# Feed-forward as seven block products for both pairs, with the output products spread between the blocks

## What is computed

```python
def swiglu_ffn(h, w1, w3, w2):
    return (jax.nn.silu(h @ w1) * (h @ w3)) @ w2
# h: 512 x 1024; w1, w3: 1024 x 2816; w2: 2816 x 1024
# x = x + gate * swiglu(...)   (first block, with a gate per channel)
# h = h + swiglu_ffn(...)      (second block, two layers)
```

## Time and profile before

| | |
|---|---|
| median of three runs | 2142.71 us (2135.99 to 2143.28) |
| span of the profiled execution | 2133.8 us |
| its own time around the span | not shown; the three runs lie 2.2 to 9.5 us above the span |
| PE busy | 2112.2 us, 99% |
| DVE busy | 1199.0 us, 56% |
| ACT busy | 949.7 us, 45% |
| POOL busy | 906.6 us, 42% |
| mean granted TensorE clock | 0.998 |

### The profile page before, as it was taken

The page is one execution under the profiler, slowest core; times in us unless marked ns, Lnnn a source line. Parts: engine busy times, 40 slices in busy tenths (PEclk is TensorE's granted clock), DMA queues, the critical chain, the costliest instruction groups (busy, mean ns, idle before and its releaser), DMA issues.

```text
span 2133.8 us, 32541 instructions
## 1 busy us (share of the span) xinstructions
PE 2112.2 (99%) x11677; PEld 1779.1 (83%) x11677; DVE 1199.0 (56%) x1776; ACT 949.7 (45%) x1519; POOL 906.6 (42%) x489
## 2 busy tenths in 40 slices
PE   8999999999999999999999999999999999999997
PEld 6888888888888988988878988988888878988986
DVE  3216545643468513546977642753788877742753
ACT  3415555743244423344464432444666754432342
POOL 3332333344435354554754454444333334454443
PEclk9999999999999999999999999999999999999999
DMA  8222222166542232333132233333222122233332
GB/s 311 80 60 60 80 79 69 55 220 210 172 152 89 85 113 89 104 92 114 50 90 89 89 105 98 102 88 110 80 80 79 54 71 83 89 109 95 111 85 73
DMA packets 63826, 216.60 MB, mean 102 GB/s; under 512 B 7105, under 2 KB 8257, under 8 KB 62593
## 3 DMA queue, kind: packets, MB, share of 16 engines
q1 hardware_dynamic: 63744, 215.55, 32.4%
HBM read 213.42 MB, written 2.10 MB: 101 GB/s over the span
## 4 chain that ended last, share of the span: by engine, by line
PE 92%; DVE 3%; ACT 2%; issue 1%; DMA 1%; SPq 0%; DVEq 0%; ACTq 0%
PE ps L660 23%; PE ps L661 23%; PE ps L662 23%; PE ps L1108 4%; PE ps L1107 4%; PE ps L1106 4%; PE ps L889 1%; PE ps L890 1%; PE ps L888 1%; PE ps L983 1%; PE ps L1281 1%; PE ps L993 1%; DMA ada_w<-in_w_ada_first 1%; DMA x_res<-in_x 1%; DVE acc L2320 1%
## 5 line engine op out<-in xcount | busy, mean ns | idle before, releaser
L465 POOL TENSOR_TENSOR w_lo<-w_raw,w_hi 128x1024 fp32r<-128x1024 f32 (+2 forms) x324 | 728.4, 2261 | 874.1 <-ACT w_hi L1415 872.8
L660 PE MATMUL ps<-h_hi,w_lo 128*128 128x512 f32 x1408 | 563.8, 400 | 1.6 <-DVE h_lo L2030 1.2
L661 PE MATMUL ps<-h_lo,w_hi 128*128 128x512 f32 x1408 | 549.1, 390 | 0.0
L662 PE MATMUL ps<-h_hi,w_hi 128*128 128x512 f32 x1408 | 548.6, 390 | 0.0
L1415 ACT ACTIVATE w_hi<-w_raw 128x1024 fp32r<-128x1024 f32 (+2 forms) x324 | 311.6, 975 | 497.3 <-PE ps L662 423.8
L660 PEld LDWEIGHTS ps<-h_hi,w_lo 128*128 128x128 f32 x1408 | 264.5, 188 | 64.2 <-issue 8.4
L662 PEld LDWEIGHTS ps<-h_hi,w_hi 128*128 128x128 f32 x1408 | 264.3, 188 | 56.3
L661 PEld LDWEIGHTS ps<-h_lo,w_hi 128*128 128x128 f32 x1408 | 264.7, 188 | 52.1 <-issue 1.0
L660 PE MATMUL ps<-gu_hi,w_lo 128*128 128x512 f32 x528 | 205.5, 389 | 0.0
L661 PE MATMUL ps<-gu_lo,w_hi 128*128 128x512 f32 x528 | 205.5, 389 | 0.0
L662 PE MATMUL ps<-gu_hi,w_hi 128*128 128x512 f32 x528 | 205.4, 389 | 0.0
(11 more groups left out here) (459 smaller groups left out, 3704.9 us busy)
## 6 DMA issues: line engine op xcount, KB each, us to landing
w_raw<-in_w_ffn_in SPq DMA_DIRECT2D x132, 512.0 KB, 3.6
w_raw<-in_w_hg SPq DMA_DIRECT2D x40, 512.0 KB, 3.6
w_raw<-in_w_ffn_out SPq DMA_DIRECT2D x48, 384.0 KB, 3.2
w_raw<-in_w_conv_gate SPq DMA_DIRECT2D x32, 512.0 KB, 3.5
w_raw<-in_w_merge SPq DMA_DIRECT2D x32, 512.0 KB, 4.6
ada_w<-in_w_ada SPq DMA_DIRECT2D x32, 512.0 KB, 4.5
w_raw<-in_w_ffn_out SPq DMA_DIRECT2D x48, 320.0 KB, 2.9
w_raw<-in_w_cp SPq DMA_DIRECT2D x20, 512.0 KB, 3.6
```

The source lines that it names most:

```text
L465: pool.tensor_tensor(w_lo[s][:, 0:n], raw[s][:, 0:n], w_hi[s][:, 0:n].bitcast(F32), ALU.subtract).then_inc(lo_done[s], 1)
L660: pe.matmul(out, wl, hi, start=first, stop=False)
L661: pe.matmul(out, wh, lo, start=False, stop=False)
L662: return pe.matmul(out, wh, hi, start=False, stop=last)
```

## The change

In all three feed-forwards rounds 0 and 1 stay ordinary, and from round 2 (the third) on both pairs are made as seven block products: 18 steps, `form(r, p)`, per feed-forward, in place of 8 or 9. Each step uses the same four half banks 2, 3, 6 and 7. The output products no longer come in two halves. The products of the round two back (8 tiles of x by two hidden tiles, so 8 groups of 6 matmuls) stand in fours within the two steps of a round, two behind the fourth block product and two behind the seventh, in banks 0, 1, 4 and 5. DVE adds each to x at once. Those of the last two rounds follow behind the last step (`last_outputs`). Weights of the output product get their own buffers (`out_raw`, `out_hi`, `out_lo`). The loops over rounds are written out. The first feed-forward makes both batches of sums of h in round 0. Some semaphores are shared where there were two.

```diff
 # PE, one step
+            def form(r, p):
+                i, o, q = form_step(e, r, p), r - FIRST_FORM, Q_FFI[e] + r
+                former, fr = 1 - p, r - 1 + p
+                if e == 0:
+                    pe.wait_ge(S["ffn_sa"], 2 * pair_no(e, fr, former) + 1)
+                else:
+                    pe.wait_ge(S["ffn_scaled"], scaled(e, fr, former) + 1)
+                if i % FORM_STEPS == 0:
+                    pe.wait_ge(S["ffn_val"], pair_no(e, FIRST_FORM - 1, 1) + 1)
+                    pe.wait_ge(S["side_val"], 2 * KC + 16 * e + 16)
+                pe.wait_ge(S["side_lo"], 1 + 2 * i + 1)
+                term(p, 0, C11, block(0, 0)).then_inc(S["side_mm"], 1)
...
+                term(p, 3, C22, summed(T1)).then_inc(S["side_mm"], 1)
+                out(o, 4 * p)
+                out(o, 4 * p + 1)
+                pe.wait_ge(S["form_kept"], 3 * i + 1)
+                pe.wait_ge(lo_done[2 * p], q + 1)
+                term(p, 0, C11, block(1, 0), add=True)
...
+                term(p, 2, C21, summed(T4), add=True).then_inc(unit_done[2 * p + 1], 1)
+                out(o, 4 * p + 2)
+                out(o, 4 * p + 3)
+            def last_outputs():
+                q = Q_FFI[e] + ROUNDS
+                for half in range(2):
+                    for t in range(2):
+                        s, r = 2 * t + half, ROUNDS - 2 + t
...
+                        for n in range(4 * half, 4 * half + 4):
...
+                            mm = out_tiles(LAST_BANKS[n], n, r, w_hi[s], w_lo[s], t == 0, t == 1)
 # POOL, one step
+                    if not final:
+                        first_form(nr, np_)
...
+                    pool.tensor_tensor(f_lo[p][0], w_12[p], f_hi[p][0].bitcast(F32), ALU.subtract).then_inc(lo_done[2 * p], 1)
...
+                    pool.tensor_tensor(f_lo[p][2], w_22[p], f_hi[p][2].bitcast(F32), ALU.subtract)\
+                        .then_inc(lo_done[2 * p + 1], 1)
...
+                    third_sum_low(nr, np_)
+                    out_low(nr - FIRST_FORM, np_)
 # DVE, ordinary rounds 0 and 1
                     if (r, p) == (0, 1):
-                        batch = 1 if e else 0
-                        terms_sum(batch)
-                        terms_low(batch)
-                    if e == 0 and (r, p) == (1, 1):
+                        if e == 0:
+                            terms_sum(0)
+                            terms_low(0)
                         terms_sum(1)
                         terms_low(1)
+                    if (r, p) == (1, 0):
+                        sum_2(FIRST_FORM, 0)
+                        lows_and_sum_4(FIRST_FORM, 0)
 # DVE, one step: additions to x of the step before, sums and joins, additions, activation
+                if i % FORM_STEPS:
+                    for n in (2, 3):
+                        out_add(o + p - 1, 4 * (1 - p) + n)
...
+                for n in (0, 1):
+                    out_add(o, 4 * p + n)
                 if e:
...
+                    scale_gate(p, r)
+                    scale_up(p, r)
+                value(p, r)
+                low(p, r)
 # DVE, end of a feed-forward
+            for n in (6, 7):
+                out_add(OUT_ROUNDS - 1, n)
+            dve_resid(dve, i, last_done, lambda n: LAST_BANKS[n], gate, **norm)
```

More of the change, by code:

```diff
@@ L63, with form_step, pair_no, scaled @@
 Q_QK, Q_V, Q_GLA, Q_MERGE, Q_MIX = 0, 2, 4, 12, 20
[L64 to L112, removed]
+Q_FFI = [22, 39, 61]
+Q_CPI, Q_CPO, Q_HG, Q_HGO = 34, 37, 51, 59
+Q_END = 73
+def form_step(e, r, p):
+    return FORM_STEPS * e + 2 * (r - FIRST_FORM) + p
+def pair_no(e, r, p):
+    return 2 * (ROUNDS * e + r) + p
+def scaled(e, r, p):
+    return 4 + 2 * (pair_no(e, r, p) - 2 * ROUNDS) if e else 2 * p
+def gu_at(r, p):
+    return 2 * (r % 3) + p
+def out_unit(e, o, n):
+    return OUT_COUNT * e + 8 * o + n
 KB = 1024
@@ L471, in pool_rounds @@
                     pool_lo(pool, s, q, sizes[s])
[L473 to L505, removed]
@@ L1162, in pe_ffn, with out_tiles @@
-            first()
-            for half, (r0, r1) in enumerate(HIDDEN):
-                for r in range(max(r0, 1), WINO_FROM[e][half]):
-                    hidden(r, h_ready(pe, h_base + KC) if (e, r) == (0, 1) else None)
-                with pe.Fori(WINO_FROM[e][half], r1) as r:
-                    winograd(half, r, r + (q_hidden(e, r0) - r0))
-                output(half)
+            def out_tiles(bank, n, r, hi, lo, first, last):
+                for t in range(2):
+                    w, g = slice(t * (D // 2) + n % 4 * P, t * (D // 2) + n % 4 * P + P), gu_at(r, t)
+                    pe.matmul(ps[:, bank, :], lo[:, w], gu_hi[:, g, :], start=(first and t == 0), stop=False)
+                    pe.matmul(ps[:, bank, :], hi[:, w], gu_lo[:, g, :], start=False, stop=False)
+                    mm = pe.matmul(ps[:, bank, :], hi[:, w], gu_hi[:, g, :], start=False, stop=(last and t == 1))
+                return mm
@@ L1674, in act_high, with columns_ahead, act_resid @@
             act.activation(tile(h_hi if out is None else out, n), x[:, n, :], ACT.Copy, scale=gain).then_inc(S["h_hi"], 1)
[L1676 removed]
+        def columns_ahead(q0):
+            return [[(n % 4, q0 + n // 4 + 1)] for n in range(KC)] + [[]]
+        def act_resid(act, i, resid_base, ahead, gain=None, twice=False, out=None):
             for n in range(KC):
[L1679 to L1682 removed]
+                for s, q in ahead[n]:
+                    act_hi(act, s, q)
                 act.wait_ge(S["resid_x"], resid_base + n + 1)
@@ L1693, in act_resid @@
                        .then_inc(S["norm_sq"], 1)
+            for s, q in ahead[KC]:
+                act_hi(act, s, q)
         def act_rms(act, i):
@@ L1828, in act_ffn @@
-            act_resid(act, i, q_out(e, 1), resid_base, 2, sizes, last, gain, twice)
+            for r in range(FIRST_FORM):
+                hidden(r)
+            for r in range(FIRST_FORM, ROUNDS):
+                for p in range(2):
+                    form(r, p)
+            for s in (2, 3):
+                act_hi(act, s, q + ROUNDS)
+            n = q + ROUNDS + 1
+            ahead = [[(0, n)], [], [], [], [(2, n), (1, n)], [], [], [], [(3, n)]]
+            act_resid(act, i, resid_base, [[]] * (KC + 1) if last else ahead, gain, twice)
@@ L1964, in _ @@
         def _(act):
-            full = [D] * 4
             act_start(act)
@@ L2478, in hidden @@
                     else:
                         if e:
-                            scale_gate(p, r, q)
-                            scale_up(p, r, q)
-                        value(p, r, q)
-                    if p and next_wino:
-                        sums(half, r + 1, q + 1)
-                        lows(half, r + 1)
+                            scale_gate(p, r)
+                            scale_up(p, r)
+                        value(p, r)
+                    if (r, p) == (1, 0):
+                        sums_3_1(FIRST_FORM, 0)
```

665 lines of the change are left out of this document (333 added, 332 removed).

## The result

The changed kernel took 2181.9 us (median of 4 runs, 2180.8 to 2183.0), the kernel before 2141.0 us on the same chip (4 runs): ratio 1.020, 95% interval 1.018 to 1.021. Forecast were 2159 us and 2137 to 2180. The direction was right; the time lies above the range, at the rival "DVE sets the steps" (2183 us). The profiled execution has a span of 2180.6 us, 46.8 us over the one before.

What follows compares the result with a forecast made beforehand. The prediction took TensorE, busy 99% of the span, as the bound, provided DVE, ACT and POOL deliver in time. -21.3 + 20.4 + 6 + 10.9 = +16 us gave a span of 2150 and, with 8.9 more, 2159 us; range 2137 to 2180.

Steps and rivals of the forecast that it cites:

- DVE sets the steps: Rival: all 36 steps of the second and third feed-forward take 16.4 instead of 15.56 us, 2183 us; chance 0.17.
- PE's own work: Matmul time: 28 more pairs as seven block products save 22.4 us, less 1.1 for changes of kind: -21.3 us.
- The entries: First block product of each feed-forward waits for DVE's value of round 1's second pair: 11, 4.7 and 4.7 us, +20.4.
- The steps: DVE's queue, blocked by POOL at the shared port, against PE's 15.56 us step: 3 us each in second and third, +6.
- The ends: Last outputs of each feed-forward: next stage waits for `h_lo` 7.1 and 3.8 us, third 0; +10.9, bounds 0 and 15.
- The last step of the sum: From the predicted span of 2150 us to the median of the runs: 8.9 us added, giving 2159 us.

Runs made afterwards that it cites:

- the tenth run: Changed kernel with POOL's output remainder later, round 2 as units, sums behind the next addition, reordered entry sums, ACT's end weights one by one: 2131.2 us, ratio 0.9969.
- experiment 4: Changed kernel with POOL's output remainder later, `gu_lo` behind the additions, and 48, 20 and 19 unused matmuls in PE's entry stalls: 2155.9 us.

## Why the prediction was too low

- **PE's own work**, -21.3: right. Block products stay at 1.44 us, a step that waits for nothing is 15.56 us, and the second feed-forward of the tenth run, with 16 such steps in place of 9, is 5.3 us shorter than before; by the sum it is 7 x (0.80 - 0.04) = 5.3.
- **The entries**, +20.4: right, 11.5, 4.8 and 4.5 = 20.8 us. In the first, two errors cancel: DVE issued the two values at 677.6 and 684.0, against 676.6 and 676.6 + 5.9 = 682.5 in the sum, and PE's wait began at 673.2, against 672.3.
- **The steps**, +6: this term failed. The mechanism and its price stood in the prediction: DVE's own 11.6 us and 4.8 of port gave 16.4 if all five POOL instructions are met; measured are 11.45 + 4.85 = 16.30, with four of them in DVE's way. What failed is the choice of 3 us per feed-forward between the bounds 0 and 14. From the trace the term is 11.4 + 9.5 in the 17 steps and 0.1 in each last one, 21.1 us. A queue that needs more than PE's step loses 0.74 us every step once its lead is used, and two to three microseconds of lead are four steps of eighteen; 2 x (17 x 0.74 - 2.5) = 20 us could have been written down. I treated "where the queues settle" as open. In the trace they settle where most instructions meet, in the first few steps: DVE's blocked instruction ends 0.54 us behind POOL's, POOL's next one, begun meanwhile, lasts 1.74 to 1.81 instead of 1.29 us, and DVE's next with two SBUF operands runs into that. Why they settle there and not elsewhere is not shown.
- **The clock** had no term. Each stall was priced at its own length; the first steps cost 5.8 us more, and experiment 4 gave 6.6 back.
- **The ends**, +10.9: 9.7 and 2.1 us of waiting, 11.8, of which the last was put at 0. It came from the square and the sum of the last tile. Behind the first two the clock is low again. From start to start, between the last output product and the same matmul some 60 places behind it, the first end costs 10.3 us more than before (988.00 to 1012.79 against 981.52 to 995.97) and the second 5.8 (1505.08 to 1524.89 against 1477.21 to 1491.27); the third costs 2.2 to the next matmul. Together 18.3 us, some 6 of them no waiting. That these 6 are the clock is an argument from its rows (0.63 to 0.79) and the 0.43 us spacing; no run filled the idle time there.

The measured terms are -21.3 + 20.8 + 21.1 + 5.8 + 18.3 = 44.7 us; the spans differ by 46.8. Of the 2 us that are left, 1.0 arises in the first 30 us, where the kernels are alike; the other was not traced.

The last step of the sum hid a part of the miss. It added 8.9 us to the span for the distance to the median. But every execution of the kernel before in these experiments lies 2.05 to 2.16 us above its own span, so the profiled one took about 2136 us, as the fastest of the three did, and most of the 8.9 is the distance between a fast execution and the median. With the 46.8 us of the spans the same sum would give 2189.5, not 2181.9; the medians differ by 41.0.

Of the rivals, "DVE sets the steps" names what happened, but its 2183 us are near 2181.9 by luck: it had 30 us for the steps instead of 21.1, nothing for the clock, and the same 8.9. I gave it 0.17, though its own price per step agreed with the earlier trace rows, where both DVE instructions beside POOL are blocked.

## What to carry over

Price a queue per period: if its own work and its meetings add up to more than the other engine's step, the loss is periods times the difference less the lead, and it is there from the first few steps on. A single wait that holds an off-path instruction until the shared port is idle can be worth about as much as the arithmetic that a change saves (20.8 against 21.3 us here), and an order with less waiting in it can be a longer one when it moves into a collision. A stall costs its length and then the slow restart behind it, and each new place in a queue of ACT, DVE or POOL has to be read for what already stands ahead of it.

## What was not expected of the hardware

PE came out of idle times of 4.5 to 11.5 us at its lower level, 1.2 GHz (granted 0.50 to 0.66 on average in the rows above, 1.00 being 2.4 GHz), and matmuls of which nothing is used, put into the idle time, took that away. Shorter idle times had it too: the clock was 0.64 behind the 2.8 us of the tenth run, and 0.59 from 1514 to 1516 us behind two of 1.76 and 1.78 in the changed kernel. At that level the 256-column matmuls start 0.21 us apart. The Trainium skill (TensorE: Matmul & The Clock Gate, Wait — 56ns, not 53.3ns?) gives columns / 1.2 GHz there, 0.213 us; the trace agrees, whereas at the full clock its 0.109 is below the 0.120 of the earlier trace rows. And two queues that block each other can fall into one rhythm: in the steady steps the durations repeat from step to step to 0.01 us.
